# Paired attention of the second block: one value product per head pair over all query tiles, scores and turned blocks in shared banks

## What is computed

```
for l in range(DEPTH):                       # 2 layers
    x = layer_norm(ALPHA * x + 0.5 * swiglu(x, ...))
    m = token_mix(x, w_in[l], w_out[l], ...)
    x = layer_norm(ALPHA * x + m)
    x = layer_norm(ALPHA * x + 0.5 * swiglu(x, ...))

# in token_mix: 8 heads of width 64, 2 key/value groups, T = 512
s_s = einsum('bqgrd,bgqkd->bgrqk', qb, k_sel);  o_s = einsum(softmax(masked s_s), v_sel)
s_w = einsum('bqgrd,bkgd->bgrqk', qb, k_win);   o_w = einsum(softmax(masked s_w), v_win)
o = gates[0] * o_c + gates[1] * o_s + gates[2] * o_w
```

## Time and profile before

| what | value |
|---|---|
| three runs | 3061.01, 3062.09, 3062.24 us, median 3062.09 |
| profiled execution | 3061.59 us |
| its span | 3059.7 us |
| TensorE clock granted over it | 0.995 of full speed |

### The profile page before, as it was taken

The page is one execution under the profiler, slowest core; times in us unless marked ns, Lnnn a source line. Parts: engine busy times, 40 slices in busy tenths (PEclk is TensorE's granted clock), DMA queues, the critical chain, the costliest instruction groups (busy, mean ns, idle before and its releaser), DMA issues. The chain is left out here.

```text
span 3059.7 us, 43808 instructions
## 1 busy us (share of the span) xinstructions
PE 2996.1 (98%) x17636; PEld 2522.5 (82%) x17636; DVE 1879.6 (61%) x2718; ACT 1284.3 (42%) x2007; POOL 1082.8 (35%) x794
## 2 busy tenths in 40 slices
PE   8999999999999999999999999999999999999998
PEld 6887878788777789987867899978998776789996
DVE  8476244837524277854475777657785447577774
ACT  4356442436553243423473534324342347443432
POOL 2443445525353422224341332242222444133222
PEclk8999999999999999999999999999999999999999
DMA  6223315313231233322210233223322221023321
GB/s 272 100 84 110 100 44 198 138 59 111 96 110 46 83 114 104 104 80 79 82 42 29 104 104 104 97 76 114 104 102 82 77 83 42 29 104 104 104 97 49
DMA packets 57441, 287.63 MB, mean 94 GB/s; under 512 B 6776, under 2 KB 7288, under 8 KB 30200
## 3 DMA queue, kind: packets, MB, share of 16 engines
q1 hardware_dynamic: 54000, 269.30, 24.7%
q10 hardware_dynamic: 3240, 15.53, 1.6%
HBM read 282.64 MB, written 2.16 MB: 93 GB/s over the span
## 5 line engine op out<-in xcount | busy, mean ns | idle before, releaser
L152 POOL TENSOR_TENSOR w_parts<-w_raw,w_parts 128x512 fp32r<-128x512 f32 x376 | 536.0, 1457 | 723.4 <-ACT w_parts L141 698.0
L421 PE MATMUL PS<-x_parts,w_parts 128*128 128x512 f32 x2688 | 668.3, 394 | 1.6 <-ACT m_all L1424 1.6
L421 PEld LDWEIGHTS PS<-x_parts,w_parts 128*128 128x128 f32 x2688 | 500.6, 188 | 113.4 <-issue 9.6
L2169 POOL TENSOR_TENSOR partial_parts<-ffn_buffers,partial_parts 128x512 fp32r<-128x512 f32 x128 | 184.5, 1443 | 746.7 <-ACT partial_parts L2364 746.7
L2210 PE MATMUL PS<-hidden_parts,partial_parts 128*128 128x512 f32 x1536 | 372.7, 391 | 0.0
L2210 PEld LDWEIGHTS PS<-hidden_parts,partial_parts 128*128 128x128 f32 x1536 | 280.1, 188 | 53.4
L2190 PE MATMUL PS<-x_parts,w_parts 128*128 128x512 f32 x1152 | 264.8, 390 | 1.0 <-POOL x_parts L873 1.0
L2190 PEld LDWEIGHTS PS<-x_parts,w_parts 128*128 128x128 f32 x1152 | 215.2, 188 | 50.4 <-POOL x_parts L873 1.9
L141 ACT CAST w_parts<-w_raw 128x2048 fp32r<-128x2048 f32 (+1 forms) x92 | 170.6, 1854 | 161.7 <-PE PS L421 73.8
L2228 PE MATMUL PS<-x_combined_parts,w_parts 128*128 128x256 f32 x1536 | 204.2, 282 | 0.2
L2228 PE MATMUL PS<-x_parts,w_parts 128*128 128x256 f32 x1536 | 204.3, 282 | 0.0
(11 more groups left out here) (442 smaller groups left out, 5009.6 us busy)
## 6 DMA issues: line engine op xcount, KB each, us to landing
w_raw<-in_w_gu SPq DMA_DIRECT2D x88, 1024.0 KB, 4.8
w_raw<-in_w_in SPq DMA_DIRECT2D x70, 1024.0 KB, 4.8
ffn_buffers<-in_w_part SPq DMA_DIRECT2D x128, 256.0 KB, 2.7
w_raw<-in_w_out SPq DMA_DIRECT2D x24, 1024.0 KB, 4.8
m_all<-in_w_next SPq DMA_DIRECT2D x14, 1024.0 KB, 8.3
w_raw<-in_w_last SPq DMA_DIRECT2D x12, 768.0 KB, 4.2
m_all<-in_w_gate SPq DMA_DIRECT2D x8, 1024.0 KB, 4.9
ssd_buffers<-decay_rows ACTq DMA_DIRECT2D x16, 512.0 KB, 3.8
```

Source lines behind the costliest of these rows:

```text
L152: pool.tensor_tensor(self.part(parts, u, 1, at, to), raw[:, self.slot(u), at:to], self.part(parts, u, 0, at, to).bitcast(F32), ALU.subtrac ...
L421: return pe.matmul(PS[0:m, self.bank(j), :], w[w_][:, k, c:c + m], part(x_, k), start=start, stop=stop)
L2169: pool.tensor_tensor(small_parts[:, d % 2, 1, :], small_raw[:, d % 2, :], small_parts[:, d % 2, 0, :].bitcast(F32), ALU.subtract).then_inc ...
```

## The change

1. Scores and turned blocks of a step share a pair of banks; three pairs (banks 0 to 5) go round by s % 3. The turned blocks of step s overwrite its scores. Turn no longer waits for a copy; score(s) waits, from s = 3, for both copies of step s - 3, and score(2) for the two banks of the compressed attention.
2. The turned blocks of a whole group stay in SBUF, ordered by key block. The two buffers are two places by group (n % 2): one takes the place of the old pt and of the buffers of the compressed attention, the other is RAW. A step with two tiles now needs two copies for each b.
3. Weigh runs once for each group: eight products of 512, 384, 256 and 128 columns for b = 0 and 1 (16 records), in place of twenty of 128 columns (40 records). It stands in PE's step 3, 6, ... 21 behind the score, and at the end for the last group.
4. Pieces of the norm come after steps 0, 2, ... 14; spread and `scale` of the first branch after steps 15, 17, 19 and 21; the four casts of `take_output` with groups 1, 2, 3 and 5.
5. The last two units of output weights are requested only after the last weigh, and copies from step 3 on wait until RAW is free.

```diff
+            def bank(self, s, b):
+                return 2 * (s % 3) + b
+            def turned_tile(self, s, b, i):
+                region = self.pt[s // 3 % 2][b]
+                return region[:, i * P:i * P + (i + 1) * 3 * P].rearrange("p (t c) -> p t c", c=3 * P)[:, :, 0:P]
+            def copy(self, eng, op, s, b):
+                eng.wait_ge(self.turned, 2 * s + b + 1)
+                if s == 3:
+                    eng.wait_ge(*self.lowered)
+                if s >= 6:
+                    eng.wait_ge(self.weighted, s // 3 - 1)
+                for _, i, at in self.tiles_of(s):
+                    last = op(self.turned_tile(s, b, i), split3(PS[:, self.bank(s, b), at:at + (i + 1) * P], i + 1))
+                last.then_inc(self.copied[b], 1)
...
             def score(self, pe, s):
-                if s >= 2:
-                    pe.wait_ge(self.smax, 2 * self.before(s - 1))
+                if s == 2:
+                    pe.wait_ge(self.emptied, 2)
+                for b in range(2):
+                    if s >= 3:
+                        pe.wait_ge(self.copied[b], s - 2)
...
             def turn(self, pe, s, b):
...
-                if s >= 1:
-                    pe.wait_ge(self.copied[b], s)
-                else:
-                    pe.wait_ge(self.emptied, b + 1)
...
-            def weigh(self, pe, s):
...
+            def weigh(self, pe, n):
+                pe.wait_ge(self.copied[0], 3 * n + 3)
+                pe.wait_ge(self.copied[1], 3 * n + 3)
...
+                    pe.wait_ge(self.taken, n)
+                w, j = divmod(n, NT)
+                for t in range(NT):
+                    for b in range(2):
+                        at = (3 * t + t) * P
+                        last = pe.matmul(PS[64 * b:64 * b + 64, 6, t * P:T], self.vf(w, j // 2, t),
+                                         self.pt[n % 2][b][:, at:at + T - t * P],
+                                         start=(t == 0), stop=(t == NT - 1), skip_group_check=True)
...
-                    if s >= 1:
-                        self.weigh(pe, s - 1)
+                    if s and s % 3 == 0:
+                        self.weigh(pe, s // 3 - 1)
                     after(s)
-                self.weigh(pe, self.steps - 1)
+                self.weigh(pe, self.steps // 3 - 1)
...
+            NORMED, SCALED, MIXED = range(0, 16, 2), range(15, 22, 2), (1, 2, 3, 5)
...
-                    act.wait_ge(att.weighted, 3 * (n + 1))
+                    act.wait_ge(att.weighted, n + 1)
...
                 def _(sp):
                     n = len(stream.units)
+                    sp.wait_ge(att.weighted, att.steps // 3)
                     stream.send(sp, RAW, n)
```

More of the change, by code:

```diff
@@ L600, in score @@
                         r = slice(64 * b, 64 * b + 64)
-                        last = pe.matmul(PS[:, 2 * (s % 2) + b, at:at + n], self.q[r, j, i * P:(i + 1) * P],
+                        last = pe.matmul(PS[:, self.bank(s, b), at:at + n], self.q[r, j, i * P:(i + 1) * P],
                                          self.kd[r, w, j // 2, 0:n], start=True, stop=True)
@@ L607, in turn @@
                 pe.wait_ge(self.prob, 2 * self.before(s) + (b + 1) * n)
-                if s >= 1:
-                    pe.wait_ge(self.copied[b], s)
-                else:
-                    pe.wait_ge(self.emptied, b + 1)
                 for t in range(self.blocks(s)):
-                    last = pe.transpose(PS[:, 4 + b, t * P:(t + 1) * P],
+                    last = pe.transpose(PS[:, self.bank(s, b), t * P:(t + 1) * P],
                                         self.p[:, s % 2, b, t * P:(t + 1) * P], ident)
                 last.then_inc(self.turned, 1)
-            def weigh(self, pe, s):
-                pe.wait_ge(self.copied[0], s + 1)
-                pe.wait_ge(self.copied[1], s + 1)
-                if s == 0:
+            def weigh(self, pe, n):
+                pe.wait_ge(self.copied[0], 3 * n + 3)
+                pe.wait_ge(self.copied[1], 3 * n + 3)
+                if n == 0:
                     pe.wait_ge(self.emptied, 3)
[L622 to L630, removed]
+                else:
+                    pe.wait_ge(self.taken, n)
[6 more added lines that the diff above has]
+                                         start=(t == 0), stop=(t == NT - 1), skip_group_check=True)
                 last.then_inc(self.weighted, 1)
@@ L655, in scalar @@
             def scalar(self, act, take):
[L656 to L661, removed]
                 for s in range(self.steps):
@@ L665, in scalar @@
                         self.exponentials(act, s)
-                        copy(s - 1)
+                        self.copy(act, act.copy, s - 1, 1)
                     if s >= 2 and (s - 1) % 3 == 0:
                         take(act, (s - 1) // 3 - 1)
-                copy(self.steps - 1)
+                self.copy(act, act.copy, self.steps - 1, 1)
                 take(act, self.steps // 3 - 1)
@@ L695, in vector @@
                         maximum(s + 1)
-                    copy(s)
+                    self.copy(dve, dve.tensor_copy, s, 0)
                     after(s)
@@ L2649, in mix_tokens @@
             v = split3(take(1024), 4)
-            pcs = take(1024)
-            pc = split3(pcs, 4)
-            pct = split3(take(1024), 2)
+            pcs_and_turned = take(2048)
+            pc, pct = split3(pcs_and_turned[:, 0:1024], 4), split3(pcs_and_turned[:, 1024:2048], 2)
             vbd = split3(take(512), 2)
@@ L2702, in mix_tokens @@
                                   lambda w, g, t: v[:, t, w * P + g * HD:w * P + (g + 1) * HD],
-                                  (pair(0), pair(1), nm, None))
+                                  (pair(0), ((over[:, 4 * T:8 * T], pcs_and_turned),
+                                             (RAW[:, 0, :], RAW[:, 1, :])), nm, None))
             def row_sum(s, h):
@@ L2707, in row_sum @@
                 return rs[:, w, i, 2 * j + h:2 * j + h + 1]
-            att.rs, att.emptied = row_sum, s_cf
+            att.rs, att.emptied, att.lowered = row_sum, s_cf, (stream.low, stream.split(10 + SLOTS))
             factor = lambda w, j: (7, 2, 3, 4)[j] if w else 7
@@ L2941, in after @@
                                   start=True, stop=True).then_inc(s_pm, 1)
-                    if s >= att.per + 3 and s - att.per - 3 < 4:
-                        if s == att.per + 3:
+                    if s in SCALED:
+                        if s == SCALED[0]:
                             pe.wait_ge(s_pw, 2)
-                        spread_coefficients(0, s - att.per - 3)
+                        spread_coefficients(0, SCALED.index(s))
                 att.tensor(pe, after)
@@ L3077, in take_output @@
                                        scale=p2("pool_s")[:, n:n + 1]).then_inc(s_pw, 1)
[L3078 to L3082, removed]
+                    if n in MIXED:
+                        k = order[MIXED.index(n)]
+                        if k < 6:
+                            act.wait_ge(s_pw, k - 3)
+                        else:
+                            act.wait_ge(s_fin, NT * (k - 5))
                         act.copy(XS[:, 0, k, :], M[:, k, :]).then_inc(parts.high, 1)
@@ L3201, in after @@
                 def after(s):
[L3202 to L3203 removed]
+                    if s in NORMED:
+                        t, c = divmod(NORMED.index(s), NT)
                         at = slice(c * P, (c + 1) * P)
@@ L3212, in after @@
                         coefficients(0)
-                    if s >= att.per + 3 and s - att.per - 3 < 4:
-                        scale(0, s - att.per - 3)
+                    if s in SCALED:
+                        scale(0, SCALED.index(s))
                 att.vector(dve, after)
```

8 lines of the change are left out of this document (1 added, 7 removed).

## The result

| | before | after |
|---|---|---|
| median, us (5 runs each, one chip) | 3062.09 | 3076.89 |
| lowest to highest | 3060.74 to 3064.11 | 3074.69 to 3077.19 |
| span of the profiled execution | 3059.7 | 3073.5 |
| granted clock over the span | 0.995 | 0.993 |

The ratio is 1.0047, interval 1.0036 to 1.0058. The forecast was 3071, slower; the measured time lies inside the range of 3057 to 3079, near its upper end. Of the step from 3062 to 3077 the sum had 9 of 15 us.

What follows compares the result with a forecast made beforehand. PE, busy 98% of the span, was taken as the bound, with chains through ACT and DVE in the attention. Profiled 3061.6 plus 9.0 for two layers gave 3070.6, median 3071 us; range 3057 to 3079.

Steps and rivals of the forecast that it cites:

- the sum: Attention, eight stretches from turn to turn: 77.5 us against 73.0, 4.5 more a layer, 9.0 in all.
- The chain: Attention: ACT's output copy waits for the joined weigh, delaying exponentials and turns; worked through eight stretches, 77.5 us a layer.
- the record count: Weigh: 16 records instead of 40 gain nothing by themselves; only two changes of piece are saved, 0.34 us a group.
- the last stretch: From turn 21 to the last spreads: 12.6 us against 7.5, as maximum(23) waits behind scale and the last weigh follows.
- The groups with a cast: Steps 9 to 14, two groups with a cast in ACT's output copy: 8.5 us each against 8.3.
- PE-paced: Rival: ACT and DVE stay ahead, PE's own work sets 65.7 us a layer; half that gain gives 3055; chance 0.14.
- the floor: PE's own work in the attention without waits: 65.7 us a layer, 7.3 less.
- Cancelling: Rival: the tail costs 5 us but the five stretches between come out 0.8 shorter each; 3063; chance 0.17.
- Cost per record: Rival: short products carry a hidden overhead that fewer records save, nearly cancelling the loss; 3061.5; chance 0.05.
- Late weights: Rival: the last two output weight transfers take over 15 us together and arrive 5 us late; 3081; chance 0.04.

Runs made afterwards that it cites:

- g1: The changed kernel with two extra products, result unused, after step 22 where PE waits for exponentials; 3069.84 us, ratio 1.0029.
- g9: The kernel before with only the shared banks, group buffers with their copies and late transfers of the change; 3057.36 us, ratio 0.9991.
- g7: The changed kernel with the weigh done step by step and spreads and scales back after steps 15 to 18; 3052.92 us, ratio 0.9972.
- g3: The changed kernel with the weigh done step by step again, all else kept; 3058.18 us, ratio 0.9990.
- g11b: The kernel before with only the spreads and scales moved to steps 15, 17, 19 and 21; 3069.14 us, ratio 1.0026.
- g6: The changed kernel, joined weigh kept, with spreads and scales back after steps 15 to 18; 3073.14 us (4 runs), ratio 1.0048.
- g2: The changed kernel with the spread and pooling product ahead of the weigh in the same step; 3067.09 us, ratio 1.0019.
- g10b: The changed kernel with DVE's scale one step later, joined weigh and spreads in place; 3066.05 us, ratio 1.0016.

## Why the prediction was right, and what it missed

**Direction and mechanism: right.** The chain gave 77.5 us a layer. With the clock held up (g1) it is 77.9 in both layers, and no stretch is off by more than about 0.3. The lump cost 2.3 us at full clock, the record count gained nothing, DVE waited 3.65 us for the spread after step 21 (3 to 4 forecast), PE 2.07 before turn 23 (some 2).

**Missed: the clock.** The step that failed is the price of the last lump and of the spreads behind it: the last stretch was put at "10.3 + 2.3 = 12.6", and the sum took the spreads at their old length. In the first layer they took 4.3 and 4.55 us, as the granted clock fell to 1.2 GHz after PE had been waiting on and off for 3 us. The price of the clock on these two pieces was put at nothing; it measured 3.0 and 1.7 us in the two layers, and g1 took it away. A second fall, after step 17 of the second layer, cost another 1.5, so that the clock makes 6.2 in all. I had read a clock of 1.00 before and carried it over to an end in which I myself had placed 2 + 1 us of waiting. None of the rivals had the clock in it either: that the time still fell inside the range is owed to the range's width, not to the working. By the traces 4.7 of the 6 us by which the forecast of 3071 was too low are this price.

**Small misses.** The groups with a cast took 8.76 and 8.80, not 8.5: ACT's wait comes back a step later at the next exponentials of 512. With two such stretches in two layers this is 1.1 us. The chain's 9.9 us (77.9 less 73.0, twice) and the clock's 6.2 give 16.1, and the profiled spans differ by 13.8; the difference is mostly that the attention of the first layer began 1.8 us earlier in the profile after, which no edit explains; among the profiles of the other kernels this start lies anywhere from 1558 to 1571.

**What each part costs.** From kernel to kernel, in medians: banks, buffers, copies and late transfers -3.4 (g9), norm pieces -4.4 (g7), late spreads +5.3 (g3), the lump +18.7 (after). That is 16.2 together, against 14.8 to 16.0 measured. By the ratios the four are -2.8, -5.8, +5.5 and +17.4, each good to some 3 to 4 us. They hold in this order only: the late spreads cost 8.0 on the kernel before (g11b), 1.6 of it clock, and 0 to 4 in the runs with the lump in place (g6). My working put the loss in the right stretches, but it set the whole new kernel against the old one. So it did not show that banks and norm pieces alone gain 8 us (g7), and that the lump costs 17 to 19: in every group from step 3 on, at the end and by the clock.

**Rivals.** PE-paced: not seen in the changed kernel, since ACT's queue waits for the lump; the floor was never near. Cancelling: the stretches of steps 9 to 14 lost 0.5 a group instead of gaining. Cost per record: excluded by g3. The Trainium skill (TensorEngine Tiling (Array Packing), Performance Considerations) puts about 60 cycles on each matmul; in g3 records of 128 columns follow each other at (1.02 - 0.80) / 4 = 55 ns, which leaves some 2 ns beside the columns, so the traces do not bear it out as a cost that adds to each record. Late weights: excluded by the rounding's row, whose wait PE ends, and by g7, which keeps the late transfers and has the lowest median.

**Open.** What decides whether the clock falls is not settled by these runs: at the end of the first layer it stayed at 1.00 in g2 and g10b and fell in g6, though PE waits in all three. Nor do the waits alone decide it: in g2 the two layers have the same waits before the last lump (0.76, 0.33 and 0.68 us), and only the second runs it at half clock. The same holds for the last step of g11b, and in the changed kernel the two layers differ in where the clock fell. The last lump of g2, first and second layer:

```profile
1633.88 2.37 PE L648 MATMUL PS<-w_raw,mixer_buffers 128*64 128x512 f32 x16 [0.68 <-issue]
2632.39 3.93 PE L648 MATMUL PS<-w_raw,mixer_buffers 128*64 128x512 f32 x16 [0.68 <-issue]
```

## What to carry to other kernels

Joining many short pieces of an engine's work into one lump saves only the changes between pieces (0.17 us each here, and less where the neighbours are alike: the lump takes 2.31 us up to a turn, 2.20 up to a spread, which has its tile form of 128*64); price against it every engine whose queue holds an instruction that waits for the lump, and what stands behind that instruction. At the drained end of a pipeline, filler work is what hides latency: keep small pieces for it, and put no late side job ahead of the last step on the engine that must feed it. Where a forecast leaves the matrix engine waiting for some us, price what follows at half clock too, as a second value beside the first, and test it with a filler.

## What was not expected of the hardware

At the end of the first layer the granted clock went to half after PE had been busy for 1.24 and 0.55 of 2 us, and was back only after some 6 us of unbroken work, so that the loss (2.1 us on the lump, 0.9 on the spreads) came to as much as the 3.1 us of waiting before it. The other seven falls in these profiles were shorter and cost 1.5 to 1.7 us each. No long wait was needed for one: in g2 the waits in the 9 us before the fall are 0.76, 0.33 and 0.68 us. Two products more in each layer, 1.7 us of useless work, made the kernel 5.5 to 7 us faster.
